# Small float32 products of a kernel's preparation moved from the whole TensorE array to four column tiles of it, then transposed

## What is computed

```python
def s5_group(u, a_re, a_im, log_dt, b_re, b_im, c_re, c_im, d_skip, glu_w, glu_b):
    lam = lax.complex(a_re, a_im)
    dt = jnp.exp(log_dt)[:, None]
    lam_bar = jnp.exp(lam * dt)
    b_bar = ((lam_bar - 1.0) / lam)[..., None] * lax.complex(b_re, b_im)
    bu = jnp.einsum('blgc,gpc->blgp', ug, b_bar)
    # h[t] = lam_bar * h[t-1] + bu[t], by an associative scan over the sequence
    y = jnp.einsum('blgp,gcp->blgc', h, lax.complex(c_re, c_im)).real + d_skip * ug
    ...
for l in range(DEPTH):
    x = x + 0.5 * swiglu(rmsnorm(x, norm_ffn1[l]), ffn1_w_in[l], ffn1_w_out[l])
    z = rmsnorm(x, norm_mix[l]) @ mix_w_in[l]
    ...
    x = x + y @ mix_w_out[l]
    x = x + 0.5 * swiglu(rmsnorm(x, norm_ffn2[l]), ffn2_w_in[l], ffn2_w_out[l])
```

## Time and profile before

| | us |
|---|---|
| median of 3 runs | 966.54 |
| lowest and highest | 964.22, 966.83 |
| the profiled execution | 965.84 |
| its span in the trace | 964.1 |
| PE busy | 945.8 |
| DVE, ACT, POOL busy | 551.7, 474.4, 377.2 |

### The profile page before, as it was taken

How to read it: one execution, slowest core, us unless ns; L and a number is a source line. 1 busy time by engine, 2 the same in 40 slices (tenths; PEclk the granted TensorE clock), 3 DMA queues, 4 the chain that set the end, 5 groups by cost and what they waited for, 6 DMA issues and landing times.

```text
span 964.1 us, 11957 instructions
## 1 busy us (share of the span) xinstructions
PE 945.8 (98%) x4594; PEld 790.9 (82%) x4594; DVE 551.7 (57%) x620; ACT 474.4 (49%) x678; POOL 377.2 (39%) x586
## 2 busy tenths in 40 slices
PE   8999999999999999999999999999999999999996
PEld 7788888878888888888888888888888888888885
DVE  3655665347967556564356555554678665555543
ACT  5544544337566444444355444443574564445432
POOL 4588998854603589998651000000034100000000
PEclk9999999999999999999999999999999999999998
DMA  7866555424237655555436655555533355566551
GB/s 228 235 207 196 188 175 178 172 92 171 88 103 227 194 180 175 178 188 202 142 121 202 191 176 192 200 175 184 177 120 132 118 188 175 175 187 222 179 175 45
DMA packets 129673, 165.11 MB, mean 171 GB/s; under 512 B 17736, under 2 KB 109008, under 8 KB 129616
## 3 DMA queue, kind: packets, MB, share of 16 engines
q1 hardware_dynamic: 129296, 163.80, 53.1%
q10 hardware_dynamic: 320, 0.53, 0.2%
HBM read 163.27 MB, written 1.05 MB: 170 GB/s over the span
## 4 chain that ended last, share of the span: by engine, by line
PE 72%; POOL 16%; DVE 3%; issue 2%; DMA 2%; ACT 2%; SPq 1%; DVEq 0%; POOLq 0%; ACTq 0%
PE bank L367 22%; PE bank L369 21%; PE bank L368 21%; POOL pt L1126 4%; POOL sc L1126 4%; POOL sc L1129 2%; DMA raw<-in_ffn_w_in 2%; POOL bp L1126 2%; PE bank L425 1%; PE bank L562 1%; PE bank L576 1%; DVE w_lo L900 1%; PE bank L501 1%; POOL cw L1132 1%; PE bank L380 1%
## 5 line engine op out<-in xcount | busy, mean ns | idle before, releaser
L900 DVE TENSOR_TENSOR w_lo<-raw,w_hi 128x1024 fp32r<-128x1024 f32 x304 | 386.1, 1273 | 340.2 <-ACT w_hi L700 340.2
L700 ACT ACTIVATE w_hi<-raw 128x1024 fp32r<-128x1024 f32 x304 | 321.1, 1060 | 317.3 <-PE bank L369 300.7
L367 PE MATMUL bank<-w_hi,x_hi 128*128 128x512 f32 x864 | 343.8, 398 | 5.1 <-DVE w_lo L900 2.2
L369 PE MATMUL bank<-w_hi,x_lo 128*128 128x512 f32 x864 | 337.2, 390 | 0.0
L368 PE MATMUL bank<-w_lo,x_hi 128*128 128x512 f32 x864 | 336.6, 390 | 0.0
L367 PEld LDWEIGHTS bank<-w_hi,x_hi 128*128 128x128 f32 x864 | 162.3, 188 | 38.3 <-issue 2.5
L369 PEld LDWEIGHTS bank<-w_hi,x_lo 128*128 128x128 f32 x864 | 162.1, 188 | 34.9
L368 PEld LDWEIGHTS bank<-w_lo,x_hi 128*128 128x128 f32 x864 | 162.5, 188 | 31.8
L1135 POOL TENSOR_TENSOR rstd_c<-ms_c,neg_half 128x2 f32<-128x2 f32 (+1 forms) x8 | 9.4, 1178 | 395.3 <-DVE ms_c L920 395.3
L367 PE MATMUL bank<-w_hi,h_hi 128*128 128x512 f32 x352 | 138.6, 394 | 0.0
L369 PE MATMUL bank<-w_hi,h_lo 128*128 128x512 f32 x352 | 137.2, 390 | 0.0
(11 more groups left out here) (145 smaller groups left out, 678.6 us busy)
## 6 DMA issues: line engine op xcount, KB each, us to landing
raw<-in_ffn_w_in SPq DMA_DIRECT2D x174, 512.0 KB
raw<-in_ffn_w_out SPq DMA_DIRECT2D x44, 1024.0 KB
raw<-in_mix_w_in SPq DMA_DIRECT2D x12, 1024.0 KB
raw<-in_mix_w_out SPq DMA_DIRECT2D x8, 1024.0 KB
raw<-in_ffn_w_in SPq DMA_DIRECT2D x4, 256.0 KB, 4.2
x<-in_x SPq DMA_DIRECT2D x12, 64.0 KB, 3.7
out<-x SPq DMA_DIRECT2D x6, 128.0 KB, 2.2
ws_raw<-in_gm_w_s SPq DMA_DIRECT2D x2, 256.0 KB
```

What stands on the lines that cost most here:

```text
L367: mm(o, hi_a, hi_b, start=first, stop=False)
L369: return mm(o, lo_a, hi_b, start=False, stop=last)
L700: A(w_hi[:, n % RING, :], raw[:, s, (n % 2) * 1024:(n % 2) * 1024 + 1024], ACT.Copy).then_inc(hi_done, 1)
L900: TT(w_lo[:, n % RING, :], raw[:, s, (n % 2) * 1024:(n % 2) * 1024 + 1024], w_hi[:, n % RING, :].bitcast(F32), ALU.subtract).then_inc(lo_d ...
```

## The change

The eight products of a group swap their operands. Now `cw` is stationary, with 32 columns, and `w1` moves, with 128 columns. The result of quarter q goes to PSUM partitions 32q to 32q + 31 by `tile_position=(0, 32 * q)`, and the loops run over r outside and q inside. The result is the transpose of the one that is wanted. So ACT copies it to a new tile `m_raw`, and PE transposes that (`m_turn`) at the start of the next group, or behind half row 19 for the last group. ACT copies the turned block into `m_sb` one group later. The number of `prep_ev` events of a layer rises from 7 to 8, and two waits on it move. POOL makes the last doubling of the tables ahead of its wait for the last group. The rows and the columns of the products' results, their number and their values are otherwise the same.

```diff
-PREP = 7
+PREP = 8
...
+        m_raw = sb("m_raw", [P, P])
...
+            def m_turn(o_m):
+
+                return nc.tensor.transpose(o_m[:, 0:P], m_raw[:, :], ident[:, :])
+
+            def prep_group(p, n, o_w, o_x, o_m):
                 pe.wait_ge(prep_ev, p * PREP + 3 + n)
+                if n:
+                    m_turn(o_m)
                 pe.wait_ge(w1_done, p * 4 + n + 1)
...
-                for q in range(4):
-                    for r in range(2):
-                        ins = mm(o_m[:, q * 32:(q + 1) * 32],
+                for r in range(2):
+                    for q in range(4):
+                        ins = mm(o_x[32 * q:32 * q + 32, 0:P],
+                                 cw[:, r, n * 4 + q, 0, :, :].rearrange("p g c -> p (g c)"),
                                  w1[:, r, q].rearrange("p s g c -> p (s g c)"),
-                                 cw[:, r, n * 4 + q, 0, :, :].rearrange("p g c -> p (g c)"),
-                                 start=r == 0, stop=r == 1)
+                                 start=r == 0, stop=r == 1, tile_position=(0, 32 * q))
...
+                    if f < DEPTH and k == FT - 3:
+                        pe.wait_ge(prep_ev, f * PREP + PREP - 1)
+                        m_turn(bank[2 * t0]).then_inc(prep_mm, 1)
...
+                if n:
+                    m_copy(n - 1, o_m)
+                A(m_raw[:, :], o_x[:, 0:P], ACT.Copy).then_inc(prep_ev, 1)
...
+                make_tables(32, NC)
+
+                pool.wait_ge(tables_done, p + 1)
                 pool.wait_ge(prep_ev, p * PREP + PREP)
...
                 pool.wait_ge(msb_done, p + 1)
-                make_tables(32, NC)
```

More of the change, by code:

```diff
@@ L452, in last_rows, with stage_end @@
                         ins.then_inc(acc_done, 1)
-            def stage_end(l, h, a_of, pairs, nxt):
+            def stage_end(l, h, a_of, pairs, nxt, prep=None):
                 for q in range(2):
@@ L463, in stage_end @@
                 last_rows(l, h, a_of, pairs, 0, 1, False)
+                if prep is not None:
+                    pe.wait_ge(prep_ev, prep * PREP + PREP - 1)
                 x_turn(*nxt, 0, 0)
@@ L467, in stage_end @@
                 last_rows(l, h, a_of, pairs, 1, 1, False)
+                if prep is not None:
+                    pe.wait_ge(prep_ev, prep * PREP + PREP)
                 x_turn(*nxt, 1, 0)
@@ L490, in prep_ws @@
                 ins.then_inc(prep_mm, 1)
-            def prep_group(p, n, o_w, o_m):
+            def m_turn(o_m):
+                return nc.tensor.transpose(o_m[:, 0:P], m_raw[:, :], ident[:, :])
+            def prep_group(p, n, o_w, o_x, o_m):
                 pe.wait_ge(prep_ev, p * PREP + 3 + n)
+                if n:
+                    m_turn(o_m)
                 pe.wait_ge(w1_done, p * 4 + n + 1)
@@ L537, in ffn @@
                             pe.wait_ge(hlo_done, UB * f + UB)
-                        prep_group(f, n, (bank[2 * c0], bank[2 * c0 + 1]), bank[2 * t0])
-                if f < DEPTH:
-                    pe.wait_ge(prep_ev, f * PREP + PREP)
+                        prep_group(f, n, (bank[2 * c0], bank[2 * c0 + 1]), bank[2 * t0 + 1], bank[2 * t0])
+                    if f < DEPTH and k == FT - 3:
+                        pe.wait_ge(prep_ev, f * PREP + PREP - 1)
+                        m_turn(bank[2 * t0]).then_inc(prep_mm, 1)
                 pe.wait_ge(hlo_done, UB * f + UB)
                 nxt = (l, 1) if j == 0 else (l + 1, 0) if l + 1 < DEPTH else None
-                stage_end(l, DNS[j] + FT - 2, lambda q: (h_hi[:, FT - 2 + q, :], h_lo[:, FT - 2 + q, :]), pairs, nxt)
+                stage_end(l, DNS[j] + FT - 2, lambda q: (h_hi[:, FT - 2 + q, :], h_lo[:, FT - 2 + q, :]), pairs, nxt,
+                          f if f < DEPTH else None)
             def in_block(l, b, part):
@@ L762, in prep_ws, with m_copy, prep_group @@
                   o.rearrange("p (i n j) -> p i j n", i=HEADS, j=T), ACT.Copy).then_inc(prep_ev, 1)
-            def prep_group(p, n, o_w, o_m):
+            def m_copy(n, o_m):
+                return A(m_sb[:, n * 4:n * 4 + 4, :], o_m[:, 0:P].rearrange("p (q m) -> p q m", q=4), ACT.Copy)
+            def prep_group(p, n, o_w, o_x, o_m):
                 q = slice(n * 4, n * 4 + 4)
@@ L768, in prep_group @@
                     A(eb[:, q, k, :], o_w[k].rearrange("p (q m) -> p q m", q=4), ACT.Copy)
-                A(m_sb[:, q, :], o_m[:, 0:P].rearrange("p (q m) -> p q m", q=4), ACT.Copy).then_inc(prep_ev, 1)
+                if n:
+                    m_copy(n - 1, o_m)
+                A(m_raw[:, :], o_x[:, 0:P], ACT.Copy).then_inc(prep_ev, 1)
             def ffn(l, j):
@@ L793, in ffn @@
                             prep_group(f, GROUP_AT[f].index(h - 4 * UB - 3),
-                                       (bank[2 * c0][:, :], bank[2 * c0 + 1][:, :]), bank[2 * t0])
+                                       (bank[2 * c0][:, :], bank[2 * c0 + 1][:, :]), bank[2 * t0 + 1], bank[2 * t0])
+                        if h - 4 * UB - 3 == FT - 3:
+                            act.wait_ge(prep_mm, f * PREP + PREP)
+                            m_copy(3, bank[2 * t0]).then_inc(prep_ev, 1)
             def mix(l):
```

## The result

| | us |
|---|---|
| before, median of 13 runs | 966.83 (964.22 to 970.11) |
| changed, median of 13 runs | 960.72 (959.14 to 963.36) |
| ratio changed to before | 0.9925, 95% interval 0.9911 to 0.9940 |
| profiled execution, changed | 961.23 (before 965.84) |

The change makes the kernel 0.6 to 0.9% faster, by the interval some 6 to 9 us, where I had predicted 2.3. The medians are 6.1 us apart, and the two profiled executions 4.6 us.

The account below looks back on a forecast made before the run. PE was taken as the bound, busy 945.8 of 964.1 us. Six groups saving 2.94 us less 0.66 for turns gave 2.3, so 964.2 us against the median of 966.54; range 960.5 to 969.5.

Parts of the forecast that it names:

- The price of the products: PE, products of a group: 1.22 us with borders in place of 1.71, so six groups save 2.94 us.
- the term of 0.90 us a group: PE, swapped products: only neighbouring passes on different tiles overlap, one 113 ns step per product, eight a group.
- the rival of all four tiles at once: PE, products: four tiles stream together, 0.45 us plus 0.32 for borders a group, time 961.5 us; chance 0.17.
- The borders: PE, switching from full array to tiles and back: 0.16 us of lost overlap each, 0.32 us a group.
- The drain: PE, change of tiling mode: the skill's drain rule spoke against the change; without border cost the gain was 4.2, not 2.3.
- Where a saved microsecond counts: PE's groups: two of layer 0 and four of layer 1 count in full; POOL waits swallow two of layer 0.
- 3.4 us of slack: Layer 1, third group: POOL's copy into `w1` ends at 476.67, 3.4 us before PE needs it at 480.07.
- the rival that the waits take the gain there: Layer 1: waits for POOL take the gain as in layer 0, time 966.5 us; chance 0.10.
- The turns: PE, eight new `m_turn`s: 0.11 us each, six outside the waits, 0.66 us lost.
- ACT's extra copy: ACT, one more copy a group: about 0.3 us, hidden by four halves of ring ahead of PE; uncovered 2.4 us.
- the 0.4 us of waits for `x`: PE, residual's transposes: two waits for DVE, all PE could win from moving POOL's tables; none counted.
- The clock: PE's clock was granted in full through a wait of 1.51 us; half a microsecond longer was taken to keep it.

Follow-up runs that it names:

- split: Changed kernel with groups at their places, POOL making less of the tables between its copies into `w1`: 956.95 us, ratio 0.9870 to the kernel before.
- the kernel before with later groups: Kernel before with groups at later half rows, its wait for the last group moved to the residual's first transposes, tables unmoved: 962.25 us, ratio 0.9940.

## Why the prediction was right and wrong

**The price of the products: the step that failed.** The step was the term of 0.90 us a group. I wrote: "The next product uses another tile, so its first pass can begin as soon as the second pass ahead of it has begun. That makes one step of 113 ns for each product, 8 x 0.113 = 0.90 us a group." I took this "because the trace shows that PE keeps passes in order and overlaps neighbours". The trace of before had all its passes on one full array, and could not say what happens on tiles. In place of 0.90 + 0.32 = 1.22 us a group's products held PE for 0.57. The runs showed that each tile works off its own passes and that the four go side by side, in either order of the program that was tried: 0.57, 1.02 and 1.87 us on four, two and one tile, and 0.59 with the loops turned round. What I had as the rival of all four tiles at once was right, with its 0.45 us of streaming. The 113 ns for 128 columns, worked out from the 225 ns of 256, was right to a few ns: the doubled products give 0.44 us for four waves, 0.11 each.

**The borders.** I took 0.32 us a group, and they cost about 0.25. Of this 0.10 us lies ahead of the first product, in the stretch that I had priced at its old value. By the measured sizes the saving of a group is 1.04 us and not 0.49; the longer first step of the next half row takes 0.02 of it back.

**The drain.** The rule of the Trainium skill (TensorEngine Tiling (Array Packing), section Key Properties) that a change of the tiling mode drains the engine agrees in part with the trace: the weight loads ahead of and behind the products show gaps of 0.17 and 0.20 us. It was no reason to expect little, since the gain of a group is four times as large.

**Where a saved microsecond counts.** That two groups of layer 0 count and two don't was right. POOL's copies begin within 0.2 us of where they did, and PE's waits grew by 0.94 and 0.92 us. In layer 1 I counted on 3.4 us of slack, and the rival that the waits take the gain there had only 0.10. In the profiled execution it took 1.52 us, in another execution of the same kernel 0.22. I had set the slack against nothing, though even by my own numbers PE would come 2 x 0.49 - 2 x 0.11 = 0.8 us earlier within the layer, and by the measured ones it came 1.9 earlier. The rest was POOL's chain, which is not a fixed clock: a pair of copies into `w1` takes 1.28 us in one place and 2.17 in another, and the chain up to the third copy took 158.5 us in the first profile of the changed kernel and 156.3 in the second.

What goes with the stretching can be read in the traces. At the second group of layer 1, DVE and POOL:

```profile
464.50 1.46 DVE L921 TENSOR_TENSOR w_lo<-raw,w_hi 128x1024 fp32r<-128x1024 f32 x1 [0.61 <-ACT w_hi L713]
```

```profile
464.94 1.49 POOL L1329 COPY w<-bp 64x512 f32<-64x512 f32 x1
```

The copy began while DVE made a `w_lo`, and ended 0.5 us behind it. In the 13 profiles 34 of the 208 copies into `w1` began while an instruction of DVE that writes `w_lo` was running, and each of them took 1.49 to 1.66 us; the other 174 took 0.60 to 0.62. Of POOL's elementwise instructions of 128 by 256 in the same profiles, all 499 that began while DVE made a `w_lo` took 1.47 us or more, and 911 of the other 931 took less than 1. No run moves the two engines' work apart, so this is a reading of the traces and not yet an experiment.

**The sum, with measured sizes.** Six groups at 1.04 us are 6.2, less six turns at 0.10 is 5.6. The new wait takes 1.5. The residual's second transposes come 1.83 us behind the first, and came 2.19 behind them before, 0.36 a layer: 0.7.

```profile
213.55 0.60 PE L380 MATMUL bank<-ident,x 128*128 128x128 f32 x4
...
215.74 0.66 PE L380 MATMUL bank<-ident,x 128*128 128x128 f32 x4 [0.20 <-DVE x L910]
```

5.6 - 1.5 + 0.7 = 4.8 us against 4.6 in the profiled pair. With a wait of 0.2 us it is 6.1, the distance of the medians. That agreement is in part luck, since both medians hold runs in which the clock fell, and the sum has no term for it. Of the distance to my 2.3 us, the products make 3.3 (six times 1.04 for 0.49), the wait takes 1.5 and the residual gives 0.7.

**The rest.** The turns cost what I said. ACT's extra copy and its extra wait are hidden as forecast; the last copy, the split held up behind it and the one ahead stand in ACT's timeline:

```profile
207.15 0.30 ACT L787 ACTIVATE m_raw<-bank 128x128 f32<-128x128 f32 x1
...
209.07 0.28 ACT L778 ACTIVATE m_sb<-bank 128x128 f32<-128x128 f32 x1 [0.69 <-PE bank L499]
209.24 1.06 ACT L713 ACTIVATE w_hi<-raw 128x1024 fp32r<-128x1024 f32 x1
```

The wait at 209.07 is 0.69 us, and no wait of PE follows from it. The tables end at 211.3 (forecast 211.7) and `m_sb` at 214.6 (forecast 215.0). I had counted none of the 0.4 us of waits for `x`; they are gone, some of it by the move of the tables.

**The clock.** I wrote that a wait longer by half a microsecond keeps the clock. It did in the first profile, through 2.12 and 2.43 us. It did not in others: in layer 0 the clock fell behind 2.12 us in the second profile of the changed kernel and in that of two tiles, behind 2.42 us in that with the loops turned round, and behind 2.91 us in the kernel with only the tables moved.

## What to carry to other kernels

When small products leave most of the array's columns unused, count the passes for each column tile and not the passes in all: on this kernel the time was the passes of one tile at the streaming time of a pass, plus some 0.25 us for the way in and out. It pays where the streaming of the swapped operand costs about what the full weight load did, and where the turned result has somewhere to go. And ask at once which wait swallows the gain: here cutting another engine's work finer, without any change to the products, took the ratio from 0.9925 to 0.9870, four to five microseconds beside the six or seven of the change itself.

## What the runs showed that I had not expected

- Column tiles take up their own passes out of the program's order: sixteen float32 passes, four in a row for each tile, took 0.59 us, and in turns 0.57 us, where taking them up in order could not have been under 1.36.
- Waits of 2 to 3 us on PE cost more than their length in some executions, because the granted clock falls to its lower level behind them. In the 112 runs of the kernels with waits of 1 us or more at their groups for which the clock is known, 57 had a mean granted clock of 0.995 or less. In the 26 runs of the four kernels without a wait above 0.8 us there, 2 had. The mean does not say where the clock fell: in four profiles (loops turned round, one tile, split, and the kernel before with later groups) it also fell for 3.4 us near 27 us, behind a wait of 1.9 to 2.3 us for DVE's `w_lo`. In the profile of the kernel with the moved tables the lower level lasted 10.2 us.
- Whether POOL's copy into `w1` took 0.6 or 1.5 us went, in all 208 cases of the 13 profiles, with whether DVE was writing `w_lo` when it began. With POOL's chain longer or shorter, a wait of PE behind it was 1.5 us in one execution and 0.2 in another of the same kernel.
- The lower clock explains much of the spread of the kernel before. In the four comparisons its 13 runs at 0.992 or less took 968.6 to 971.8 us, and its 9 runs at 0.998 or more took 964.5 to 967.1.
